# Second attention: probabilities turned by VectorE and stored and loaded, instead of turned by TensorE; first attention: scores wait for their own heads

## What is computed

```
scores = jnp.einsum("bnqkgd,bnjkd->bnkgqj", qb, kw).astype(jnp.float32) * scale
scores = jnp.where(valid[None, :, None, None, :, :], scores, -jnp.inf)
m = jnp.maximum(jnp.max(scores, axis=-1), sink)
p = jnp.exp(scores - m[..., None])
denom = jnp.sum(p, axis=-1) + jnp.exp(sink - m)
probs = (p / denom[..., None]).astype(v.dtype)
out = jnp.einsum("bnkgqj,bnjkd->bnqkgd", probs, vw)
```

## Time and profile before

| | |
|---|---|
| median of three runs | 1289.55 us |
| the profiled execution's own time | 1289.76 us |
| its span in the profile | 1288.0 us |
| TensorE busy with products | 1278.0 us (99%) |
| VectorE busy | 852.3 us (66%) |
| ScalarE busy | 598.0 us (46%) |
| GpSimd busy | 86.2 us (7%) |
| moved by DMA | 138.67 MB |

### The profile page before, as it was taken

How to read it: one execution, slowest core, us unless ns; L and a number is a source line. 1 busy time by engine, 2 the same in 40 slices (tenths; PEclk the granted TensorE clock), 3 DMA queues, 4 the chain that set the end, 5 groups by cost and what they waited for, 6 DMA issues and landing times.

```text
span 1288.0 us, 15494 instructions
## 1 busy us (share of the span) xinstructions
PE 1278.0 (99%) x5879; PEld 1030.6 (80%) x5879; DVE 852.3 (66%) x1146; ACT 598.0 (46%) x875; POOL 86.2 (7%) x68
## 2 busy tenths in 40 slices
PE   9999999999999999999999999999999999999998
PEld 7887777888888888888888888888877777778886
DVE  6489799899868676666665335574467878445444
ACT  6234466232363443333333224413379899544223
POOL 0000222000000200000000002200012220000000
PEclk9999999999999999999999999999999999999999
DMA  8456122432322232322222222369622121222421
GB/s 291 149 132 164 66 66 66 163 99 93 104 97 68 98 98 98 98 98 98 98 98 98 98 98 68 129 128 242 189 74 70 66 83 66 98 67 98 163 66 66
DMA packets 158505, 138.67 MB, mean 108 GB/s; under 512 B 60872, under 2 KB 137584, under 8 KB 158192
## 3 DMA queue, kind: packets, MB, share of 16 engines
q1 hardware_dynamic: 158432, 137.89, 34.4%
q10 hardware_dynamic: 16, 0.00, 0.0%
HBM read 126.87 MB, written 11.01 MB: 107 GB/s over the span
## 4 chain that ended last, share of the span: by engine, by line
PE 94%; DVE 2%; DMA 1%; SPq 1%; ACT 1%; issue 0%; ACTq 0%
PE PS L1831 92%; PE PS L1898 2%; SPq L461 1%; DVE WL L1109 1%; DMA QKT<-qk_channel_major 0%; DMA STAGE<-in_w_in 0%; DMA qk_channel_major<-QK 0%; DVE QK L1197 0%; DVE QK L1201 0%; DVE XL L1145 0%; DVE XG L1137 0%; ACT WH L662 0%; DVE SMALL L1186 0%; DVE QK L1181 0%; ACT TG L716 0%; ACT QKT L743 0%
## 5 line engine op out<-in xcount | busy, mean ns | idle before, releaser
L662 ACT ACTIVATE WH<-STAGE 128x1024 fp32r<-128x1024 f32 x214 | 225.9, 1058 | 538.5 <-PE PS L1831 526.2
L1109 DVE TENSOR_TENSOR WL<-STAGE,WH 128x1024 fp32r<-128x1024 f32 x214 | 276.3, 1293 | 167.7 <-ACT WH L662 167.0
L1831 PE MATMUL PS<-XH,WH 128*128 128x512 f32 x960 | 381.2, 397 | 0.0
L1831 PE MATMUL PS<-XH,WL 128*128 128x512 f32 x960 | 374.0, 390 | 0.0
L1831 PE MATMUL PS<-XL,WH 128*128 128x512 f32 x960 | 373.9, 389 | 0.0
L1831 PEld LDWEIGHTS PS<-XH,WH 128*128 128x128 f32 x960 | 180.3, 188 | 42.3 <-issue 4.3
L1831 PEld LDWEIGHTS PS<-XL,WH 128*128 128x128 f32 x960 | 180.4, 188 | 38.5 <-issue 2.4
L1831 PEld LDWEIGHTS PS<-XH,WL 128*128 128x128 f32 x960 | 180.2, 188 | 38.0
L1831 PE MATMUL PS<-WH,XH 128*128 128x512 f32 x224 | 88.0, 393 | 0.3 <-DVE XL L1145 0.2
L1831 PE MATMUL PS<-WH,XL 128*128 128x512 f32 x224 | 87.2, 389 | 0.0
L1831 PE MATMUL PS<-WL,XH 128*128 128x512 f32 x224 | 87.2, 389 | 0.0
(11 more groups left out here) (291 smaller groups left out, 1804.2 us busy)
## 6 DMA issues: line engine op xcount, KB each, us to landing
STAGE<-in_w_in SPq DMA_DIRECT2D x52, 1024.0 KB, 5.0
STAGE<-in_w_up SPq DMA_DIRECT2D x22, 1024.0 KB, 5.0
STAGE<-in_w_down SPq DMA_DIRECT2D x11, 1024.0 KB, 4.7
STAGE<-in_w_out SPq DMA_DIRECT2D x4, 1024.0 KB, 5.0
STAGE<-in_w_rnn_out SPq DMA_DIRECT2D x4, 1024.0 KB, 5.0
STAGE<-in_w_attn_out SPq DMA_DIRECT2D x4, 1024.0 KB, 5.1
STAGE<-in_w_o SPq DMA_DIRECT2D x4, 1024.0 KB, 4.9
XTOK<-in_x SPq DMA_DIRECT2D x4, 512.0 KB, 7.1
```

What stands on the lines that cost most here:

```text
L662: act.activation(ring(WH, n), staged(n), ACT.Copy).then_inc(hi_done, 1)
L1109: dve.tensor_tensor(ring(WL, n), staged(n), ring(WH, n).bitcast(F32), ALU.subtract)\
L1831: return pe.matmul(out_, lhsT, rhs, start=start, stop=stop, skip_group_check=True)
```

## The change

Turning the probabilities leaves TensorE. VectorE turns them in blocks of 32x32, each block staying among its 32 partitions (`window_turn`, now in VectorE's list after `lo` of unit 2w+3), into a new buffer TB. SyncE then stores TB to a buffer in HBM so that the blocks land in their places (`p_store`, four transfers in pieces of 32 values), and loads it back with keys on the partitions (`p_load`, one or two transfers), into PT with two buffers and PTK for the odd windows from 7 on. ScalarE's copy `window_pt` is gone. The values' product stands four units later, after unit 2w+8, and so does its reading; `att_hi` and `att_low` are two units later, the load of FG six STAGE transfers later. In the first attention the first scores wait for five scaled tiles (all queries and the first keys) instead of eight, and the later pairs for theirs. Two semaphores are merged with others.

```diff
@@ -235,7 +235,9 @@
...
         S2 = [at("S2A", [P, 2, 2, 256], F32, 182), at("S2B", [P, 2, 2, 256], F32, 190)]
-        PT = at("PT", [P, 2, 2, 2, P], F32, 186)
+        PT = [at("PT0", [P, 2, 512], F32, 186), at("PT1", [P, 2, 512], F32, 120)]
+        PTK = [at("PTK0", [P, 512], F32, 80.5), at("PTK1", [P, 512], F32, 88)]
+        TB = [at("TB0", [P, 1024], F32, 124), at("TB1", [P, 1024], F32, 144)]
         UP2 = at("UP2", [P, 2, 516], F32, 194)
@@ -351,6 +355,21 @@
...
             return st.rearrange("p (k c) -> p k c", k=2)[:, :, u * 512:(u + 1) * 512]
+
+        def turned(w):
+
+            n = 256 - first_key(w)
+            return TB[min(w // 7, 1)][:, 0:4 * n].rearrange("p (c k) -> p c k", k=n)
+
+        def keys_first(w, kb):
+
+            if w % 2 and w >= 7:
+                return PTK[kb][:]
+            return PT[w % 2][:, kb, :]
+
+        def parts_in(w):
+
+            return 16 * sum(2 - first_key(v) // P for v in range(w + 1))
 
@@ -450,6 +469,28 @@
...
 
+            def p_store(w):
+
+                sp.wait_ge(s2_turned, w + 1)
+                for a in range(4):
+                    sp.dma_start(PROW[w % 2].rearrange("(k j) (c a i) -> a j c k i", j=32, a=4, i=32)
+                                 [a, :, :, first_key(w) // 32:],
+                                 turned(w)[32 * a:32 * a + 32].rearrange("p c (k i) -> p c k i", i=32))\
+                      .then_inc(p_out, 16)
+
+            def p_load(w):
+
+                sp.wait_ge(p_out, 64 * (w + 1))
+                if w == 1:
+                    sp.wait_ge(x1_out, 64)
+                if w == 7:
+                    sp.wait_ge(bsq_ready, KD)
+                if w >= 2:
+                    sp.wait_ge(pv_done, w - 1)
+                for kb in range(first_key(w) // P, 2):
+                    sp.dma_start(keys_first(w, kb), PROW[w % 2][kb * P:(kb + 1) * P, :])\
+                      .then_inc(pt_in, 16)
+
             def q2_load(h):
@@ -546,9 +587,14 @@
...
                     sp.dma_start(XT2[:], XROW.rearrange("(t p) d -> p t d", p=P)).then_inc(xt2_in, 16)
-                if p == U_H // 2 + 2:
+                if p == U_H // 2 + 8:
                     sp.wait_ge(bd_done, KD)
                     sp.dma_start(FG[:], final_norm_g_2.partition_broadcast(P)).then_inc(fg_in, 16)
+                w = p - U_GR // 2 - 5
+                if 1 <= w < 17:
+                    p_load(w - 1)
+                if 0 <= w < 16:
+                    p_store(w)
             for t in range(TT):
@@ -945,15 +991,6 @@
...
 
-            def window_pt(w):
-                act.wait_ge(pt_t, w + 1)
-                if w > 0:
-                    act.wait_ge(pv_done, w)
-                kb = first_key(w) // P
-                act.activation(PT[:, kb:].rearrange("p a b c d -> p (a b c d)"),
-                               PS[:, 4 + kb:6, :].rearrange("p b c -> p (b c)"), ACT.Copy)\
-                   .then_inc(pt_ready, 1)
-
             def window_scale(w):
@@ -1006,6 +1043,10 @@
...
                 for k in ks:
+                    if k == 4:
+                        act.wait_ge(pv_done, 6)
+                    if k == 6:
+                        act.wait_ge(p_out, 64 * 7)
                     act.wait_ge(yr_ready, k + 1)
@@ -1066,8 +1105,8 @@
...
                     merge_gates(h)
-                if j in (34, 35, 36):
-                    att_hi(((0, 1, 2), (3, 4, 5), (6, 7))[j - 34])
+                if j in (36, 37, 38):
+                    att_hi(((0, 1, 2), (3, 4, 5), (6, 7))[j - 36])
                 if h >= 25:
@@ -1679,6 +1717,18 @@
...
                    .then_inc(s2_max, 1)
+
+            def window_turn(w):
+
+                dve.wait_ge(s2_ready, 4 * w + 4)
+                if w:
+                    dve.wait_ge(p_out, 64 * w)
+                else:
+                    dve.wait_ge(x1_out, 64)
+                if w == 7:
+                    dve.wait_ge(bd_done, KD)
+                dve.transpose(turned(w), S2[w % 2][:].rearrange("p a b c -> p (a b) c")
+                              [:, :, first_key(w):]).then_inc(s2_turned, 1)
 
@@ -1772,9 +1822,11 @@
...
                 drain(j)
-                if j % 2 == 0 and 4 <= j < 36:
-                    window_read(j // 2 - 2)
+                if j % 2 == 0 and 8 <= j < 40:
+                    window_read(j // 2 - 4)
                 lo(U_GR + j + 4)
+                if j % 2 and 3 <= j < 35:
+                    window_turn((j - 3) // 2)
                 if h >= 25:
@@ -1794,8 +1846,8 @@
...
                     rnn_low({18: (0, 1, 2), 20: (3, 4, 5), 22: (6, 7)}[j])
-                if j in (35, 36, 37):
-                    att_low(((0, 1, 2), (3, 4, 5), (6, 7))[j - 35])
+                if j in (37, 38, 39):
+                    att_low(((0, 1, 2), (3, 4, 5), (6, 7))[j - 37])
             merge_low(7)
@@ -1974,8 +2026,9 @@
...
                 else:
-                    pe.wait_ge(qkt_ready, 8)
                     pe.wait_ge(drained, DR_B)
+                if s % 3 == 0:
+                    pe.wait_ge(qkt_ready, KW + p + 1)
                 for jq, c0 in step_blocks(s):
@@ -2229,29 +2282,18 @@
...
 
-            def window_turn(w):
-
-                pe.wait_ge(s2_ready, 4 * w + 4)
+            def window_values(w):
+
+                g, nb = divmod(w, TT)
+                pe.wait_ge(pt_in, parts_in(w))
                 if w:
-                    pe.wait_ge(pt_ready, w)
                     pe.wait_ge(pv_read, w)
-                for kb in range(first_key(w) // P, 2):
-                    for par in range(2):
-                        for idx in range(2):
-                            c = (2 * par + idx) * P
-                            last = tr(PS[:, 4 + kb, c:c + P], S2[w % 2][:, par, idx, kb * P:(kb + 1) * P])
-                last.then_inc(pt_t, 1)
-
-            def window_values(w):
-
-                g, nb = divmod(w, TT)
-                pe.wait_ge(pt_ready, w + 1)
                 kbs = (0, 1) if nb else (1,)
...
                                   V2[:, nb - 1 + kb, g * DH:(g + 1) * DH],
-                                  PT[:, kb, par].rearrange("p i q -> p (i q)"),
+                                  keys_first(w, kb)[:, par * 256:par * 256 + 256],
                                   kb == kbs[0], kb == 1)
@@ -2273,10 +2315,8 @@
...
                     cm_unit(U_GR + j, j % 2, BHA, BLA, 0, att_parts if h == 24 else None)
-                if j % 2 and 3 <= j < 35:
-                    window_turn((j - 3) // 2)
-                if j % 2 == 0 and 4 <= j < 36:
-                    window_values(j // 2 - 2)
+                if j % 2 == 0 and 8 <= j < 40:
+                    window_values(j // 2 - 4)
                 if j % 2 == 0 and j < 32:
```

More of the change, by code:

```diff
@@ L261, in program @@
         XSCR = nc.dram_tensor("x_channel_major", [P, KD * SEQ], F32, kind="Internal").ap()
+        PROW = [nc.dram_tensor(f"probabilities{i}", [256, 512], F32, kind="Internal").ap()
+                for i in range(2)]
         QKROW = [nc.dram_tensor(f"qk_channel_major{i}", [W, SEQ], F32, kind="Internal").ap()
@@ L292, in program @@
         vec_t, vec_ready = sem("vec_t"), sem("vec_ready")
-        sgw_turned, wt_ready = sem("sgw_turned"), sem("wt_ready")
+        wt_ready = sem("wt_ready")
         xh_ready, xl_ready, sq_ready = sem("xh_ready"), sem("xl_ready"), sem("sq_ready")
@@ L318, in program @@
         fh_ready, fl_ready = sem("fh_ready"), sem("fl_ready")
-        rope_ready, q2_turned, k2_turned = sem("rope_ready"), sem("q2_turned"), sem("k2_turned")
+        rope_ready, q2_turned = sem("rope_ready"), sem("q2_turned")
         q2_out, q2t_in = [sem("q2_out0"), sem("q2_out1")], sem("q2t_in")
@@ L330, in program @@
         s2_rcp = sem("s2_rcp")
-        s2_mask, qk2_done, s2_max, s2_exp, s2_ready, pt_t, pt_ready, pv_done, pv_read = (
+        s2_mask, qk2_done, s2_max, s2_exp, s2_ready, s2_turned, p_out, pt_in, pv_done, pv_read = (
             sem("s2_mask"), sem("qk2_done"), sem("s2_max"), sem("s2_exp"), sem("s2_ready"),
-            sem("pt_t"), sem("pt_ready"), sem("pv_done"), sem("pv_read"))
+            sem("s2_turned"), sem("p_out"), sem("pt_in"), sem("pv_done"), sem("pv_read"))
         c_tap, y_tap = sem("c_tap"), sem("y_tap")
@@ L527, in _ @@
                     q2_store(1)
-                    sp.wait_ge(k2_turned, 1)
+                    sp.wait_ge(q2_turned, 2 * TT + 1)
                     for a in range(4):
@@ L1035, in _ @@
                 hi(U_GR + j + 4)
-                if j % 2 and 3 <= j < 35:
-                    window_pt((j - 3) // 2)
                 if j % 2 == 0 and 2 <= j < 34:
@@ L1239, in _ @@
                     sgw = SGW[:].rearrange("p g t -> p (g t)")
-                    dve.transpose(sgw, sgw).then_inc(sgw_turned, 1)
-                    dve.wait_ge(sgw_turned, 1)
+                    link(dve.transpose(sgw, sgw))
                     dve.tensor_tensor(WT[:], SGW[:], MINC[:].unsqueeze(1).broadcast_to([P, 8, P]),
@@ L1646, in _ @@
```

(7 more changed lines are left out.)

2 lines of the change are left out of this document (removed).

## The result

| | before | changed | ratio |
|---|---|---|---|
| median | 1289.49 us (1289.16 to 1289.63, 5 runs) | 1281.51 us (1281.44 to 1283.33, 5 runs) | 0.9945, 95% interval 0.9934 to 0.9955 |
| own time of the profiled execution | 1289.76 us | 1281.51 us | |
| span | 1288.0 us | 1279.8 us | |

The change makes the kernel faster, by 8.25 us in the profiled executions. The five times fall into two groups, 1281.4 to 1281.5 us (mean granted clock 0.999 to 1.000) and 1282.9 to 1283.3 us (0.998), for a reason that no profile shows; the median and the profiled execution belong to the first. The prediction had 1276.5 us and a range to 1281.0; the time lies 0.5 us above that range. Predicted were 13.06 us less (1289.76 to 1276.7), so 4.8 us are missing.

A forecast was written before the change was run, and what follows sets the result against it. TensorE, busy 1278.0 of 1288.0 us, was taken as the bound. 1289.76 - 12.0 + 0.4 - 1.46 = 1276.7 us for an execution like the profiled one, so 1276.5 us as median; range 1275.0 to 1281.0.

The forecast's parts named there:

- Removed: On TensorE: 112 turns in 12 groups of eight and 4 of four leave its list, 12.0 us gained.
- Moved: On TensorE: values go four units later, so two more pairs of scores and values stand apart, 0.4 us lost.
- First scores: First attention: TensorE's wait behind ScalarE's scaling of keys vanishes, 1.46 us gained; VSG has about 0.5 us of room.
- The round trip: Probabilities through HBM: store 6.2 us, load 7.5 to 15 us against 15 available, cost 0.
- The factor 19: Skill's slowdown for turning by DMA strides: at 19 times 6.2 us a window needs 118 us, kernel some 16 x 100 more.
- The end of the stage: Last halves of BHA and BLA made in unit 39's turn, room 0.5 to 1 us; cost 0, at most 0.5.
- VectorE's turn: New turn on VectorE: 1.23 us for 128x1024, half for the 4 short windows, 17 us in all.
- Added to VectorE, removed from ScalarE: VectorE gains 17 us of turns, ScalarE loses 14 us of copies; cost 0, up to 4 us if backlogs add up.
- The step's second look: Tightest drain, unit 21's, is done 4.0 us before TensorE reaches unit 23; 2 to 3.5 us of that go.
- VectorE's list becomes the bound in the recurrence: Rival: TensorE waits at units 20 to 24 or for last BLA tiles, 1 to 5 us, 1278 to 1281.5; chance 0.17.
- the other: The case that the whole kernel goes as summed, 1275.3 to 1278 us; chance 0.62.

The follow-up runs named there:

- e1: Changed kernel with VectorE's turn placed ahead of `lo` instead of behind it, nothing else changed: 1276.29 us, ratio 0.9899 to the kernel before.
- e2: Kernel before with only the new waits of the first attention's scores: 1288.39 us, ratio 0.9993.
- e5: Kernel before with VectorE's 16 turns added behind `lo` into a buffer nobody reads, TensorE's turns kept: 1289.29 us, ratio 0.9999.
- e9: Changed kernel with VectorE's turn done twice in units 5, 9, 13 and 17: 1286.51 us, ratio 0.9980 to the kernel before.
- e10: Kernel before with VectorE's unread turns added behind `lo`, done twice in units 5, 9, 13 and 17: 1292.98 us, ratio 1.0029.

## Why the prediction was wrong

- **Removed, Moved, First scores:** right in sum. e1 has the changed kernel's work with no stall, and its profiled execution took 1276.38 us against 1276.7 in the sum. The first scores' 1.46 us were read from an execution with a long wait; the medians of e2 give 0.9. Of the 13.0 us between e1 and the kernel before (1289.27 to 1276.29) this leaves some 12.1 for the turns and their places, where the sum had 11.6: two small misses that cancel, which is luck. VSG was no wait (its product starts at 119.27, right behind the scores at 118.42, with no idle time; the step said 119.3).
- **The round trip:** the cost of 0 was right, its prices were not. A full window's four stores took 5.3 to 6.7 us to issue, not 2.8, and 5.8 to land, not 3.4; the loads took 5.6, inside the bounds. The room held: window 1's stores were issued from 961.00, its load went out at 975.28, had landed by about 982 (1.0 of issue and 5.6), and its values came at 989.01, 13.7 us after the load's issue (predicted 15). Of the two rules of the Trainium skill that spoke against this part, neither decided. The one of DMA: Bandwidth & Descriptors, Specifications, that pieces below 512 bytes are read, modified and written, may be why a store of 128 KB took longer than a load of 256 KB (5.8 against 5.6 us). No run here separates that from the company the stores had. The factor 19 of VectorE: DVE Perf Modes, The three transpose paths, did not show for runs of 32 values: a store landed in 5.8 us, and the 118 us estimated from that page did not come.
- **The end of the stage:** right, TensorE waits for no BLA tile.
- **VectorE's turn:** 1.24 us for 128x1024 and 0.70 for 128x512, predicted 1.23 and half of it.
- **"Added to VectorE, removed from ScalarE ... Cost: 0":** this step failed, and here alone the 5.0 us lie. Its numbers were nearly right: VectorE busy for 51.6 and ScalarE for 51.6 of the 60 us from 1000 (predicted 51 and 50 of 57). The step took VectorE's 13.6 us without work in 60 as room for 4.9 us more. But in the stretch before, much of the idle time is a wait for the other engine (from 957 to 1050 VectorE waits 10.1 us for ScalarE and 8.7 for TensorE): at unit 5 it had 3.09 us ahead of `lo` and none behind it. What counts is the length of the path that goes around between the two, and a turn behind `lo` is on it whole. ScalarE's relief, argued in the step as an offset, gave almost nothing back. Of the two copies of a round one had stood in ScalarE's wait for the square: that wait is 1.36 us before and 2.48 in e5, where the copy is still there, and 3.39 in the changed kernel, where it is gone: 0.91 longer, with the tap no earlier after the high part (4.43 in the changed kernel, 4.44 in e5). The other stood right behind unit 7's high part, ahead of the sigmoids ("974.63 1.01 ACT L953 ACTIVATE PT<-PS 128x1024 f32<-128x1024 f32 x1" in the kernel before). Without it the sigmoids come 0.9 us sooner after that high part (II 3.86 us behind it before, 2.94 in the changed kernel). But the way over VectorE's turn and scan to the next high part is as long as the way over the copy was (15.67 us in e9, 15.80 in e10), so the round gains 0.1 us by it.
- The step's second look, at one drain with 4.0 us of room, was at the right place: there, at unit 23, TensorE waited 1.7 us, as the rival named it ("TensorE waits at units 20 to 24"). The step let 2 to 3.5 us of the room go, and 5.7 went. It did not look at the three waits for sigmoids at units 8, 12 and 16. Nothing in the text measured the distance from a sigmoid to the gates' products.
- **The rival** "VectorE's list becomes the bound in the recurrence" came nearest, though the bound was not VectorE's list but the loop of both engines. It was given a chance of 0.17 where the other had 0.62. Its prices of 1 to 5 us gave 1278 to 1281.5. The range was cut at 1281.0, inside this rival, and the time came at 1281.51.

Could the profile before have told it? Partly. Every four units ScalarE waits 1.36 us for the square in RR, and VectorE 1.8 to 3.1 us for the high part in WH: two engines that wait for each other at fixed places are a loop, and its length without TensorE is the round less the time in which either waits for TensorE. That sum would have had to be made. The profile before does not give it as a view, since its chain lies on TensorE.

## What to carry to other kernels

When the bound engine gets shorter by 6% in a stage, look for the loop between the other engines that was just covered, not at their busy shares: follow one round of mutual waits, add the new instruction to it, and compare with the bound engine's new round. Then place the new instruction in front of the wait for the other engine, not behind what ends it. Here that is two lines exchanged, for 5.2 of 13 us. And when the likeliest rival has a price, the range should reach to its end.

## What the runs showed of the hardware

**Behind two waits of over 2 us TensorE ran at half clock, and the trace calls it work.** In e9 TensorE waited 2.18 us for II, and the four gates' products behind it took 3.65 us, where they took 1.95 in the changed kernel behind a wait of 0.91. The timeline:

```profile
977.49 3.65 PE L1886 MATMUL PS<-UC,LRUW 128*128 128x512 f32 x4 [2.18 <-ACT II L1021]
980.20 1.17 PE L1886 MATMUL PS<-XH,WH 128*128 128x512 f32 x1
981.21 0.39 PE L1886 MATMUL PS<-XL,WH 128*128 128x512 f32 x1
```

and the stretches of 1 us (busy time of each engine, then PEclk, DMA share and GB/s):

```profile
976.00:977.00 1.00, 0.00 (x0) 0.00 (x0) 1.00 (x2) 0.99 (x3) 0.00 (x0) 1.00 0.00 0
977.00:978.00 1.00, 0.51 (x1) 0.45 (x2) 0.97 (x4) 1.00 (x3) 0.00 (x0) 0.78 0.63 176
978.00:979.00 1.00, 1.00 (x2) 0.34 (x1) 0.97 (x2) 1.00 (x2) 0.00 (x0) 0.50 1.07 378
979.00:980.00 1.00, 1.00 (x2) 0.34 (x1) 1.00 (x3) 1.00 (x3) 0.56 (x1) 0.50 1.10 376
980.00:981.00 1.00, 1.00 (x3) 0.36 (x2) 1.00 (x2) 0.92 (x3) 1.00 (x2) 0.52 0.87 272
981.00:982.00 1.00, 1.00 (x6) 0.82 (x5) 1.00 (x2) 0.82 (x2) 1.00 (x1) 1.00 0.97 341
```

The granted clock is half, 1.2 in place of 2.4 GHz, until 981. The same follows the wait of 2.35 us at unit 16 (granted 0.50 from 1043 to 1045). This is why e9's waits grew less than its time: two such stretches took up about 1.7 us each (in the rows above, what PEclk lacks to 1.00, summed). Its ten executions have mean clocks of 0.996 to 0.999 and yet agree within 0.5 us, which fits a loop that sets the round while TensorE only fills the rest of it. In the profiled execution of the changed kernel waits of 1.65 and 1.70 us left the granted clock at 1.00. Why the clock fell behind the two waits of e9 and not behind these is not shown.

**VectorE's smallest instructions are long while GpSimd multiplies.** A maximum of two 128x4 operands takes 0.16 us as a rule, and this one 2.30, ending as GpSimd's product of 128x1024 ends. VectorE and GpSimd of the changed kernel:

```profile
1013.12 2.30 DVE L1716 TENSOR_TENSOR SMALL<-SMALL,SINK 128x4 f32<-128x4 f32 x1
1015.46 0.17 DVE L1717 TENSOR_SCALAR SMALL<-SMALL 128x4 f32<-128x4 f32 x1
```

```profile
1013.00 2.41 POOL L681 TENSOR_TENSOR GT<-GT,SIG 128x1024 f32<-128x1024 f32 x1
```

Such a 2.3 us instruction stands in the loop too, once a round, at 983.02, 1013.12 and 1044.36, each time beside this product of GpSimd's. The Trainium skill's SBUF — State Buffer, SBUF: two separate sides, describes a port pair that VectorE and GpSimd share, held by one of them for a whole instruction; the trace agrees (0.12 us after the start of the one, the other has to last until its end). Moving one of the two was not tried; in e1 it could bring nothing, since there the round is TensorE's.
